# A hybrid decoder layer with product-key experts: sixteen more rows of the last dense tile take their down products from gathered expert rows, and the dense down products become 336 columns wide

## The chip, the cores and the metric

The kernel runs on one core of one Trainium2 chip. The metric is the device time of one execution in microseconds (us); the time before is 1582.34 us, the median of three runs (1581.97 to 1584.03). Everything is float32; a dense product is built from three TensorE products of the operands' high and low halves (high by high, high by low, low by high).

## The reference

The layer mixes 512 tokens of width 1024 through a gated convolution and an HGRN2 recurrence, attends to 256 memory tokens, and ends with the PEER channel mixer, which is where the change lies:

```python
q = (tokens @ w_query).reshape(Ntok, 8, 2, 128)
s = einsum('nhpd,hpkd->nhpk', q, sub_keys)          # 2 x 128 sub-keys per head
s_top, i_top = top_k(s, 16)
cand = s_top[:, :, 0, :, None] + s_top[:, :, 1, None, :]
best, pos = top_k(cand, 16)                          # 16 of 16384 experts per head
gate = softmax(best)
u = take(expert_down, idx);  a = gelu(einsum('nd,nhkd->nhk', x, u))
v = take(expert_up, idx);    out = einsum('nhk,nhkd->nd', gate * a, v)
```

So every token has 8 x 16 = 128 chosen experts; each costs one dot product with a row of `peer_down` (1024 numbers) and adds one weighted row of `peer_up`.

## The kernel before

The 512 tokens are four tiles of 128. The kernel splits them by method.

**Dense tokens.** For three tiles, less the last 32 rows of the third ("edge" rows), it computes all 16384 experts densely. `DN = 384` are the tokens of the three tiles, `DE = DN - EDGE = 352` those treated densely. The *down stage* runs over 128 blocks of 128 experts: `first_product(i)` calls `columns`, which does 8 x 3 = 24 matmuls with 352 moving columns into a PSUM bank; ScalarE applies GELU. 104 blocks of results are spilled to DRAM (`hid_dram`, ScalarE's DMA queue), 24 are kept. The *up stage* (`second_product`) again runs over 128 blocks, 24 matmuls of 352 columns each; its operand is the hidden value times a gate that is zero unless the token chose that expert.

**Gates.** The dense gate matrix is built by TensorE from one-hot matrices that VectorE makes. That is the *gate stage*: `STEPS = DE // TB = 44` steps of eight tokens. In step n VectorE makes the one-hots (`hots(n)`: two comparisons, one product), TensorE runs a down block and 24 small bf16 matmuls (`gate_step(n)`), ScalarE copies two banks of gates out. Before it run `AHEAD` down blocks, while VectorE still chooses experts; after it come the remaining down blocks, here called the *tail*.

**Gathered tokens.** For the fourth tile and the 32 edge rows, the expert rows are gathered. One gathered "row" is an indirect DMA by GpSimd (`down_row(k)`), which brings one expert row for each of 128 partitions (512 KB), and one VectorE instruction (`dots`, L1250 before) that multiplies it with the token in PSUM and sums. The fourth tile needs 128 such rows; the 32 edge tokens spread over four groups of 32 partitions, so 32 more: `ROWS = 160`. `row_stream` sets the order: 32 rows of the tile, the 32 of the edge, 96 of the tile. Whenever the kind changes, VectorE rewrites the token operand in PSUM (L1246, L1249). From the gate stage on four buffers hold the rows: row k is issued once the dot of row k-4 is done.

**What sets the order.** All is written out by hand. Per down block p: SyncE loads the weights (five buffers); ScalarE writes the high half (`high(p)`, L603) once block p-3 is done, since there are three buffers; GpSimd subtracts to get the low half (`low(p)`, L470); TensorE's block p waits for it. GpSimd has only one instruction stream, so gathers and low halves alternate in an order given by tables: `DOTS_STEP` says how many rows follow each low half in the gate stage (ten steps with two, then the pattern 1, 2, 2), `DOTS_END` how many follow each in the tail. VectorE's dots in the gate stage follow the same table. Edge data move between partitions by small DMAs on ScalarE's queue: tokens (`edge_h`), expert numbers (`edge_idx`, L889), gates (`edge_gate`, L918). At step `SPLIT_AT` VectorE splits the third tile's gates into three bf16 pieces (`gate_pieces`, L1374 to L1377).

## Time and profile before

| | us |
|---|---|
| median of three runs | 1582.34 |
| profiled execution, own time | 1584.32 |
| its span | 1582.4 |
| TensorE busy | 1565.8 (99% of the span) |
| VectorE busy | 1164.6 (74%) |
| GpSimd busy | 963.6 (61%) |
| ScalarE busy | 663.3 (42%) |

The down stage begins at 512.8 us into the span, its gate stage runs from 719.0 to 949.9, the tail to about 1073, the up stage to the end. TensorE is PE, VectorE DVE, ScalarE ACT, GpSimd POOL, SyncE SP. A matmul's listed duration overlaps that of the next, so the pace of TensorE is read from the distance of two starts, not from durations. A row of the timeline gives start, duration, engine, line, operation, output<-input, count, and in brackets how long the engine had been idle and what released it.

### The profile page before, as it was taken

How to read it: one execution, taken by the hardware profiler on the slowest of the kernel's cores; microseconds unless marked ns; L12 is line 12 of the kernel's file. 1: busy time of each engine (PE TensorE's matmuls, PEld its weight loads, DVE VectorE, ACT ScalarE, POOL GpSimd, SP SyncE). 2: the span in 40 equal slices, each digit the busy share in tenths (PEclk: the TensorE clock that was granted, in tenths of full speed). 3: DMA queues.
4: the chain of work that ended last, by engine and by line, in shares of the span. 5: the costliest groups of instructions: out<-in, count | busy, mean ns of one | idle time of the engine just before them, and what ended most of it. 6: DMA issues, size and time to landing. Idle time of an engine off the chain costs nothing.

```text
span 1582.4 us, 26079 instructions
## 1 busy us (share of the span) xinstructions
PE 1565.8 (99%) x9937; PEld 1483.6 (94%) x9937; DVE 1164.6 (74%) x2263; ACT 663.3 (42%) x994; POOL 963.6 (61%) x555
## 2 busy tenths in 40 slices
PE   8999999999999999999999999999999999999997
PEld 6888888888989999999999999999999999999997
DVE  5155351251579999999999883338999999998995
ACT  5352452552434444444444544334334333333433
POOL 4463326523235899887778778876757665564741
PEclk9999999999999999999999999999999999999999
DMA  5232252313424999989999999879999999999981
GB/s 196 88 103 67 73 158 95 115 54 118 149 84 130 302 347 349 330 285 313 379 399 397 396 410 393 309 248 365 411 410 406 399 406 409 395 404 393 400 354 54
DMA packets 129697, 438.91 MB, mean 277 GB/s; under 512 B 13888, under 2 KB 28224, under 8 KB 121280
## 3 DMA queue, kind: packets, MB, share of 16 engines
q1 hardware_dynamic: 60592, 227.43, 39.6%
q0 software_dynamic: 46080, 167.79, 27.8%
q10 hardware_dynamic: 22928, 42.41, 7.0%
q8 instruction: 59, 0.97, 0.2%
q14 instruction: 38, 0.31, 0.1%
HBM read 395.21 MB, written 41.81 MB: 276 GB/s over the span
## 4 chain that ended last, share of the span: by engine, by line
PE 50%; DVE 4%; DMA 3%; issue 1%; POOL 1%; ACT 0%; ACTq 0%; POOLq 0%
PE psum L1589 16%; PE psum L1590 16%; PE psum L1591 16%; DMA arena<-down_rows,kept 3%; PE psum L1905 2%; DVE arena L1415 1%; DVE arena L1250 1%; POOL w_low L470 1%; POOL arena L502 0%; DVE arena L1410 0%; DVE arena L1411 0%; DVE arena L1323 0%; DVE kept L1375 0%; DVE arena L1383 0%; PE psum L1941 0%
## 5 line engine op out<-in xcount | busy, mean ns | idle before, releaser
L470 POOL TENSOR_TENSOR w_low<-kept,w_high 128x1024 fp32r<-128x1024 f32 x205 | 500.7, 2445 | 316.8 <-ACT w_high L603 306.1
L1589 PE MATMUL psum<-hT_high,w_high 128*128 128x352 f32 (+2 forms) x1392 | 477.6, 343 | 1.7 <-POOL w_low L470 1.7
L1591 PE MATMUL psum<-hT_high,w_low 128*128 128x352 f32 (+2 forms) x1392 | 470.6, 338 | 0.0
L1590 PE MATMUL psum<-hT_low,w_high 128*128 128x352 f32 (+2 forms) x1392 | 470.6, 338 | 0.0
L1590 PE MATMUL psum<-wgt_low,up_high 128*128 128x352 f32 x1016 | 330.0, 325 | 0.0
L1589 PE MATMUL psum<-wgt_high,up_high 128*128 128x352 f32 x1016 | 328.7, 324 | 0.0
L1591 PE MATMUL psum<-wgt_high,up_low 128*128 128x352 f32 x1016 | 327.5, 322 | 0.0
L603 ACT ACTIVATE w_high<-kept 128x1024 fp32r<-128x1024 f32 x211 | 222.6, 1056 | 129.6 <-PE psum L1591 91.2
L1589 PEld LDWEIGHTS psum<-hT_high,w_high 128*128 128x128 f32 x1392 | 262.1, 188 | 14.5 <-issue 2.9
L1590 PEld LDWEIGHTS psum<-hT_low,w_high 128*128 128x128 f32 x1392 | 262.3, 188 | 11.8 <-issue 0.5
L1591 PEld LDWEIGHTS psum<-hT_high,w_low 128*128 128x128 f32 x1392 | 262.0, 188 | 12.0
L1250 DVE CUSTOM_DVE_ANT_0 arena<-arena,psum 128x1024 f32<-128x1024 f32 x160 | 192.3, 1215 | 78.1 <-DMA arena<-down_rows,kept 77.5
L607 ACT ACTIVATE up_high<-arena 128x1024 fp32r<-128x1024 f32 x128 | 135.6, 1059 | 269.2 <-PE psum L1591 214.8
L550 POOL DMA_INDIRECT kept<-up_in,kept x100 | 175.7, 1757 | 103.3 <-DVE kept L1459 76.0
L502 POOL DMA_INDIRECT arena<-down_rows,kept x160 | 153.2, 958 | 68.9 <-DVE kept L1250 45.8
L1591 PEld LDWEIGHTS psum<-wgt_high,up_low 128*128 128x128 f32 x1016 | 193.0, 190 | 0.0
L1590 PEld LDWEIGHTS psum<-wgt_low,up_high 128*128 128x128 f32 x1016 | 191.1, 188 | 0.0
L1589 PEld LDWEIGHTS psum<-wgt_high,up_high 128*128 128x128 f32 x1016 | 190.5, 188 | 0.0
L1445 DVE TENSOR_TENSOR up_low<-arena,up_high 128x1024 fp32r<-128x1024 f32 x128 | 156.4, 1222 | 20.0 <-ACT up_high L607 19.8
L550 POOL DMA_INDIRECT arena<-up_in,kept x60 | 112.4, 1873 | 66.6 <-DVE kept L1459 48.3
L1459 DVE SCALAR_TENSOR_TENSOR kept<-kept 128x1024 f32<-128x1024 f32 x80 | 102.4, 1280 | 2.0
L1415 DVE TENSOR_TENSOR arena<-arena,psum 128x3072 bf16<-128x3072 bf16 x44 | 76.9, 1748 | 0.0
(285 smaller groups left out, 1957.3 us busy)
## 6 DMA issues: line engine op xcount, KB each, us to landing
kept<-down_in SPq DMA_DIRECT2D x128, 512.0 KB, 6.4
arena<-up_pairs SPq DMA_DIRECT2D x64, 1024.0 KB, 9.2
kept<-front_w SPq DMA_DIRECT2D x92, 512.0 KB, 3.5
gate_dram<-arena ACTq DMA_DIRECT2D x40, 512.0 KB, 11.0
arena<-hid_dram SPq DMA_DIRECT2D x52, 352.0 KB, 12.7
arena<-gate_dram SPq DMA_DIRECT2D x8, 1280.0 KB, 14.0
kept<-gate_dram SPq DMA_DIRECT2D x8, 1280.0 KB, 14.2
hid_dram<-arena ACTq DMA_DIRECT2D x52, 176.0 KB, 6.6
```

Of the source, the lines that this page charges most:

```text
L470: nc.gpsimd.tensor_tensor(lower, ring[:, p % RING, :], high.bitcast(F32), ALU.subtract).then_inc(low_ready, 1)
L502: nc.gpsimd.indirect_dma_start(ring[slot], None, down_rows, bass.IndirectOffsetOnAxis((edge_idx if edge else idx3)[:, j:j + 1].bitcast(U32 ...
L550: nc.gpsimd.indirect_dma_start(rows_c[k % RING_C], None, up_rows, bass.IndirectOffsetOnAxis(numbers.bitcast(U32), 0))\
L603: nc.scalar.activation(w_half(p)[0], ring[:, p % RING, :], ACT.Copy).then_inc(high_ready, 1)
L607: nc.scalar.activation(up_hi[:, s % 4, :], uraw[:, up_slot(s), :], ACT.Copy).then_inc(up_high, 1)
L1250: nc.vector.tensor_tensor_reduce(ring[slot], ring[slot], h_row, 1.0, 0.0, ALU.mult, ALU.add, (edge_dot if edge else dot3)[:, j:j + 1]).the ...
L1415: nc.vector.tensor_tensor(hot_g[:, s], hot_i.rearrange("p (n q) i r -> p n q i r", q=1).to_broadcast(each), pieces[:, m:m + PAIRS].rearran ...
L1445: nc.vector.tensor_tensor(up_lo[:, up_slot(s), :], uraw[:, up_slot(s), :], up_hi[:, s % 4, :].bitcast(F32), ALU.subtract).then_inc(up_low, 1)
L1459: ins = nc.vector.scalar_tensor_tensor(x[:, ST, :], row, w3[:, n:n + 1], x[:, ST, :], ALU.mult, ALU.add)
L1589: nc.tensor.matmul(out, lhs[0], rhs[0], start=first, stop=False)
L1590: nc.tensor.matmul(out, lhs[0], rhs[1], start=False, stop=False)
L1591: return nc.tensor.matmul(out, lhs[1], rhs[0], start=False, stop=last)
```

## The change

`SEMI = 16` rows ahead of the 32 edge rows of the third tile leave the dense down products, which become `DS = DE - SEMI = 336` columns wide. The dense up products stay at 352. The 16 tokens are spread over eight groups of 16 partitions, so their 128 experts are 16 more gathered rows: `ROWS` goes from 160 to 176. They stand behind the edge rows in the stream. Their tokens, numbers and results travel by 24 more small DMAs on ScalarE's queue (8 for `semi_idx` with four blocks, 8 for `edge_h`, 8 for `semi_gel` with gate steps 17 to 20). Their GELU values are multiplied into the gates before these are split into pieces (now at step 23), so the dense gate matrix holds gate times GELU for them; in the up stage ScalarE copies these 16 columns per block (`weights_tail`) in place of VectorE's product. ScalarE's loop of the up stage is written out. The tables of times are shifted: `AHEAD` from 52 to 54.

```diff
-EXP_AT = (15, 30, 45)
-PICKED_AT = 19
-TURN_AT = (PICKED_AT + 4, 36, 52)
+EXP_AT = (16, 31, 47)
+PICKED_AT = 20
+TURN_AT = (PICKED_AT + 4, 38, 54)
...
+SEMI = 16
+DS = DE - SEMI
...
+SEMI_SLOTS = SLOTS // SEMI_PARTS
+ROWS = SLOTS + EDGE_SLOTS + SEMI_SLOTS
...
-GEL_AT, SPLIT_AT, LAST_TURN = 12, 20, 28
+GEL_AT, SEMI_AT, SPLIT_AT, LAST_TURN = 12, 17, 23, 30
...
-DOTS_END = (1,) * 22 + (2,) * 5
+DOTS_END = (2,) * 20 + (1,) * 8
...
+            def weights_tail(i):
+                block = (i + SPILL) % NK
+                nc.scalar.activation(wraw[:, i % 4:i % 4 + 1, DS:DE], near[:, block:block + 1, NEAR - SEMI:NEAR], ACT.Copy)\
+                    .then_inc(tail_copied, 1)
...
             def weight_high(i, s):
+                act.wait_ge(tail_copied, i + 1)
...
             for n in range(DT):
-                early_tiles((4 + PARTS, TURN_AT[0], TURN_AT[1])[n], EXP_AT[n])
+                if n == 1:
+                    act.wait_ge(edge_moved, 2 * 16 * PARTS)
+                    for q in range(SEMI_PARTS):
+                        if q % 2 == 0:
+                            early_at(TURN_AT[0] + q // 2)
+                        act.dma_start(semi_idx[q * SEMI:(q + 1) * SEMI, :],
+                                      idx_last[SEMI0:E0, q * SEMI_SLOTS:(q + 1) * SEMI_SLOTS]).then_inc(semi_moved, 16)
+                if n == 2:
+                    act.wait_ge(dot_done, FIRST_EDGE + 1)
+                    act.wait_ge(semi_moved, 16 * SEMI_PARTS)
+                    for q in range(SEMI_PARTS):
+                        early_at(TURN_AT[1] + q)
+                        act.dma_start(edge_h[q * SEMI:(q + 1) * SEMI], hn[SEMI0:E0, DT - 1, :].rearrange("p (k n) -> p k n", k=KC))\
+                            .then_inc(semi_moved, 16)
...
+                if n == SEMI_AT:
+                    act.wait_ge(dot_done, SEMI_DONE)
+                    act.wait_ge(semi_moved, 2 * 16 * SEMI_PARTS)
+                    step(nc.scalar.activation(semi_dot, semi_dot, ACT.Gelu))
+                if SEMI_AT <= n < SEMI_AT + SEMI_PARTS // 2:
+                    for q in (2 * (n - SEMI_AT), 2 * (n - SEMI_AT) + 1):
+                        act.dma_start(semi_gel[SEMI0:E0, q * SEMI_SLOTS:(q + 1) * SEMI_SLOTS],
+                                      semi_dot[q * SEMI:(q + 1) * SEMI, :]).then_inc(semi_moved, 16)
...
                     elif k == EDGE_DONE:
                         dve.wait_ge(dot_done, k)
+                        dve.wait_ge(semi_moved, 2 * 16 * SEMI_PARTS)
+                        step.put(nc.vector.memset(semi_gel, 1.0))
+                        step(nc.vector.tensor_tensor(h_chunks, edge_h, ffn_row.rearrange("p (k n) -> p k n", k=KC), ALU.mult))
+                    elif k == SEMI_DONE:
+                        dve.wait_ge(dot_done, k)
                         step(nc.vector.tensor_copy(h_chunks, own_h))
...
+                    dve.wait_ge(semi_moved, 3 * 16 * SEMI_PARTS)
+                    step.put(nc.vector.tensor_tensor(split_last[:, 2, :], split_last[:, 2, :], semi_gel, ALU.mult))
...
-                columns(i + FRONT, hT_half, DE, 4 + i % 2)
+                columns(i + FRONT, hT_half, DS, 4 + i % 2)
```

GpSimd near the end of the down stage, before: `w_low` is the low half of a down block's weights, `down_rows` a gathered row; one row follows each low half until the last three, which have two.

```order
253 L502 DMA arena<-down_rows,kept 128x1024 [waits dot_done]
254 L470 TENSOR_TENSOR w_low<-kept,w_high 128x1024 [waits high_ready]
255 L502 DMA arena<-down_rows,kept 128x1024 [waits dot_done] x2
256 L470 TENSOR_TENSOR w_low<-kept,w_high 128x1024 [waits high_ready]
259 L502 DMA arena<-down_rows,kept 128x1024 [waits dot_done] x2
260 L470 TENSOR_TENSOR w_low<-kept,w_high 128x1024 [waits high_ready] x7
```

The same place now, where the last of the low halves with two rows behind it stands; nineteen such pairs stand before it in the tail, and four with one row behind it.

```order
249 L476 TENSOR_TENSOR w_low<-kept,w_high 128x1024 [waits high_ready]
250 L510 DMA arena<-down_rows,kept 128x1024 [waits dot_done] x2
251 L476 TENSOR_TENSOR w_low<-kept,w_high 128x1024 [waits high_ready]
252 L510 DMA arena<-down_rows,kept 128x1024 [waits dot_done]
258 L510 DMA arena<-down_rows,kept 128x1024 [waits dot_done]
259 L476 TENSOR_TENSOR w_low<-kept,w_high 128x1024 [waits high_ready] x6
```

So in the tail twenty low halves have two gathers behind them where there were three. ScalarE behind the last copy of edge numbers (block 22 before, 23 now); `kept<-kept 32x32` is that copy, before:

```order
344 L855 DMA hid_dram<-kept 128x352 [waits gelu_out]
345 L889 DMA kept<-kept 32x32
346 L603 ACTIVATE w_high<-kept 128x1024 [waits block_used,weight_slot2]
347 L853 ACTIVATE kept<-psum 128x352 [waits hid_stored3,block_used]
348 L855 DMA hid_dram<-kept 128x352 [waits gelu_out]
```

and now:

```order
347 L869 DMA hid_dram<-kept 128x336 [waits gelu_out]
348 L917 DMA kept<-kept 32x32
349 L611 ACTIVATE w_high<-kept 128x1024 [waits block_used,weight_slot3,edge_moved]
350 L867 ACTIVATE arena<-psum 128x336 [waits hid_stored0,block_used]
351 L869 DMA hid_dram<-arena 128x336 [waits gelu_out]
352 L899 DMA kept<-kept 16x16 x2
```

The next high half of weights now also waits for `edge_moved`, that is for the landing of the copy issued just before it.

## Rows read from the trace of the kernel before

**Rows 1.** PE's waits over the whole span, the longest in the down stage.
```profile
PE psum L1589 <- POOL w_low L470: 1.9, 4, 1.1
```
**Rows 2.** Timeline, PE: moving widths 256 and 352.
```profile
224.90 0.28 PE L1591 MATMUL psum<-memT_high,w_low 128*128 128x256 f32 x1
...
225.62 0.28 PE L1591 MATMUL psum<-memT_high,w_low 128*128 128x256 f32 x1
...
999.94 0.32 PE L1589 MATMUL psum<-hT_high,w_high 128*128 128x352 f32 x1
...
1003.78 0.32 PE L1589 MATMUL psum<-hT_high,w_high 128*128 128x352 f32 x1
```
**Rows 3.** Timeline: ACT and POOL in one block of the tail.
```profile
1000.14 0.46 ACT L952 ACTIVATE arena<-psum 128x352 f32<-128x352 f32 x1 [2.43 <-PE psum L1591]
...
1001.62 2.41 POOL L470 TENSOR_TENSOR w_low<-kept,w_high 128x1024 fp32r<-128x1024 f32 x1 [0.34 <-ACT w_high L603]
```
**Rows 4.** Timeline: POOL in the tail, a block with two rows.
```profile
1028.51 2.40 POOL L470 TENSOR_TENSOR w_low<-kept,w_high 128x1024 fp32r<-128x1024 f32 x1 [0.33 <-ACT w_high L603]
...
1032.31 0.94 POOL L502 DMA_INDIRECT arena<-down_rows,kept  x1 [0.30 <-issue]
1033.27 2.41 POOL L470 TENSOR_TENSOR w_low<-kept,w_high 128x1024 fp32r<-128x1024 f32 x1
```
**Rows 5.** DMA issues, gathered rows, 950 to 975 and 1030 to 1045: count, median landing.
```profile
arena<-down_rows,kept POOLq DMA_INDIRECT x7, 8.0
...
arena<-down_rows,kept POOLq DMA_INDIRECT x6, 6.6
```
**Rows 6.** Timeline: ACT at the last copy of edge numbers; line L889's landings.
```profile
602.06 0.47 ACT L853 ACTIVATE kept<-psum 128x352 f32<-128x352 f32 x1 [1.27 <-PE psum L1591]
...
602.93 0.53 ACTq L889 DMA_DIRECT2D kept<-kept  x1
...
DMA to landing us min/median/max: 4.5/5.7/6.8
```
**Rows 7.** Timeline: DVE's first operation of the gate stage.
```profile
712.65 0.36 DVE L1406 COPY psum<-arena 128x192 f32<-128x192 f32 x1 [3.40 <-ACT arena L876]
```
**Rows 8.** Timeline: how a late row reaches PE in the gate stage.
```profile
774.81 1.22 DVE L1250 CUSTOM_DVE_ANT_0 arena<-arena,psum 128x1024 f32<-128x1024 f32 x1 [1.81 <-DMA arena<-down_rows,kept]
...
777.27 2.39 POOL L470 TENSOR_TENSOR w_low<-kept,w_high 128x1024 fp32r<-128x1024 f32 x1
...
779.81 0.40 PE L1589 MATMUL psum<-hT_high,w_high 128*128 128x352 f32 x1 [1.09 <-POOL w_low L470]
```
**Rows 9.** The chain that ended last: PE's small matmuls of two gate steps.
```profile
880.01 1.39 PE psum L1905 x24
885.29 1.39 PE psum L1905 x24
```
**Rows 10.** DVE by line, 719 to 950: count, busy us, mean ns; then L1246 alone.
```profile
L1250 DVE CUSTOM_DVE_ANT_0 arena<-arena,psum 128x1024 f32<-128x1024 f32 x76 | 91.1, 1218 | 11.2 <-DMA arena<-down_rows,kept 10.8
L1415 DVE TENSOR_TENSOR arena<-arena,psum 128x3072 bf16<-128x3072 bf16 x42 | 73.4, 1748 | 0.0
...
L1249 DVE COPY psum<-arena 128x1024 f32<-128x1024 f32 x1 | 1.2, 1220 | 0.0
...
L1246 DVE TENSOR_TENSOR psum<-arena x1: 2097/2097/2097, 637.4 to 637.4; 128x1024 f32<-128x1024 f32 x1
```
**Rows 11.** Timeline: DVE at the splitting of the gates.
```profile
815.05 3.20 DVE L1375 TENSOR_TENSOR kept<-kept 128x128 f32<-128x128 f32 x1
...
818.55 0.29 DVE L1377 TENSOR_TENSOR kept<-kept 128x128 f32<-128x128 f32 x1
```
**Rows 12.** Line L918, the four copies of edge gates in the gate stage.
```profile
DMA to landing us min/median/max: 7.5/9.0/11.9
```
**Rows 13.** Windows: us; PE, PEld, DVE, ACT, POOL busy; PE clock, DMA share, GB/s.
```profile
826.00:950.00 124.00, 123.73 (x1136) 120.66 (x1134) 111.67 (x150) 60.20 (x96) 98.00 (x66) 1.00 1.02 402
...
1576.00:1577.00 1.00, 0.00 (x0) 0.00 (x0) 1.00 (x3) 0.61 (x1) 0.00 (x0) 0.50 0.00 0
```

More of the change, by code:

```diff
@@ L85 @@
 SPILL = NK - KEEP
+OWN, AT_EDGE, IN_SEMI = range(3)
 def row_stream():
-    stream, own, edge = [], 0, 0
-    for k in range(ROWS):
-        if edge < EDGE_SLOTS and k >= FIRST_EDGE:
-            stream.append((True, edge))
-            edge += 1
-        else:
-            stream.append((False, own))
-            own += 1
-    return stream
+    middle = [(AT_EDGE, j) for j in range(EDGE_SLOTS)] + [(IN_SEMI, j) for j in range(SEMI_SLOTS)]
+    own = [(OWN, j) for j in range(SLOTS)]
+    return own[:FIRST_EDGE] + middle + own[FIRST_EDGE:]
 STREAM = row_stream()
 EDGE_DONE = FIRST_EDGE + EDGE_SLOTS
+SEMI_DONE = EDGE_DONE + SEMI_SLOTS
 V_MIX, V_CONV, V_HGRN, V_LB0, V_LB1, V_ATT, V_MEM, V_FFN, V_CW = 0, 8, 12, 16, 20, 24, 32, 40, 48
@@ L498, in down_row @@
                     pool.wait_ge(dot_done, k - ahead + 1)
-                edge, j = STREAM[k]
-                if edge and j == 0:
+                group, j = STREAM[k]
+                if group == AT_EDGE and j == 0:
                     pool.wait_ge(edge_moved, 2 * 16 * PARTS)
+                if group == IN_SEMI and j == 0:
+                    pool.wait_ge(semi_moved, 16 * SEMI_PARTS)
                 nc.gpsimd.indirect_dma_start(ring[slot], None, down_rows, bass.IndirectOffsetOnAxis(
-                    (edge_idx if edge else idx3)[:, j:j + 1].bitcast(U32), 0))\
+                    (idx3, edge_idx, semi_idx)[group][:, j:j + 1].bitcast(U32), 0))\
                     .then_inc(landed[slot], 16)
@@ L1241, in dots @@
                     dve.wait_ge(landed[slot], 16 * (n + 1))
-                    edge, j = STREAM[k]
+                    group, j = STREAM[k]
                     if k == FIRST_EDGE:
```

48 lines of the change are left out of this document (25 added, 23 removed).

## The prediction, on record before the changed kernel ran

> **What bounds the kernel now.** I read the page's table first: TensorE is busy 99% of the span. In the view of waits the longest entry that concerns the down stage is 1.9 us behind GpSimd's low halves, four times [rows 1]. So the time is TensorE's work, and a column less is worth its price as long as nobody else becomes late. Next that price: six matmuls of width 256 start 0.72 us apart (120.0 ns each), 24 of width 352 start 3.84 us apart (160.0 ns) [rows 2]. That is (160.0 - 120.0) / 96 = 0.417 ns a column; at 336 columns it gives 153.3 ns a matmul and 24 x 153.3 = 3.68 us a block. Then I asked, stage by stage, who would be late behind a faster TensorE. In a tail block TensorE begins a block at 999.94, ScalarE's GELU of the last one follows 0.20 later, then the high half, and the low half runs 1001.62 to 1004.03 [rows 2, 3]. The block that needs it starts two blocks after 999.94, at 1007.62: GpSimd leads by 3.6 us and can lead by no more, since the high half waits for a finished block. In the gate stage the chain is longer: a dot that waited 1.81 us for its row ends at 776.0, GpSimd's next low half starts at 777.27, TensorE's block at 779.81 after 1.09 us idle [rows 8]. VectorE and DMA are near their limits there: even in the calmer second half of the stage VectorE is busy 111.67 of 124 us and the DMA share is 1.02 at 402 GB/s [rows 13].
>
> **The change, part by part.** The sum is made against the profiled execution, 1584.3 us (span 1582.4 and 1.9 around it), which is 2.0 above the median of the runs.
>
> *Width.* 128 blocks x 24 = 3072 matmuls lose 16 x 0.417 = 6.67 ns each: -20.5 us. Both widths of the slope bracket nothing near 336 but the line; I give this term no range.
>
> *The tail.* `DOTS_END` puts two gathers behind twenty low halves. Such a block takes GpSimd 1033.27 - 1028.51 = 4.76 us [rows 4], and the two behind it in the trace the same within 0.05; it waits for no other engine in it. TensorE will want a block each 3.68 us. Before, 22 tail blocks had one gather (2.41 for the low half and some 1.1 for the gather, hidden in 3.84), three had two, and the lead swallowed those 3 x 0.92. Now GpSimd loses 4.77 - 3.68 = 1.09 us on each of twenty, 21.8 us, of which the lead, 7.36 - 4.09 = 3.3 us at the new pace, swallows its part once: TensorE waits 18.5 us. Nothing repays it. That is the lower end. The upper end comes from the four row buffers: row k needs the dot of row k-4, so a pair of rows needs half of landing L plus dot and gaps, about (L + 1.6) / 2. With the 6.6 us at the tail's end this is 4.1, hidden; with the median of 8.0 at its start, where the spill and the last gate stores still run, it is 4.8, and 5.5 for a row that takes 9.4 [rows 5]. If all twenty blocks went at 5.5 it would be 33 us. The first six have that load; I add 2 us for them and take 20.5 (18.5 to 33).
>
> *A new wait on ScalarE, once.* After the fourth copy of edge numbers ScalarE waits until it has landed; behind that wait stand the high half of block 26, hence GpSimd's low half and TensorE's block. The copy is issued 0.87 us after the GELU starts, and such copies land after 4.5 to 6.8 us, 5.7 in the middle [rows 6]. From the start of block 24: 0.20 + 0.87 + 5.6, then high half and gap 1.12 (in rows 3 the 1.48 from GELU to low half, less 0.36 of GELU), low half 2.41: 10.2 us, where TensorE wants it at 2 x 3.68 = 7.36. Stall 2.8 us (1.7 to 4.1). Could the start of the gate stage swallow it? There VectorE waits 3.40 us for the turned indices [rows 7], so it isn't the late one, and the stall stays.
>
> *Gate steps 2 to 11.* The bubble of rows 8 falls in step 11: up to there VectorE, its rows and GpSimd set the pace, and TensorE's lead is used up. What TensorE saves by then is lost again: 12 x 0.16 = 1.9 us. VectorE also gets a product of tokens and norm gains (2.10 us for L1246) in place of the copy (1.22), and a small memset [rows 10]: +1.0. Together 2.9 us (1.9 to 4; the copy itself comes back at step 16, when VectorE gains: steps with one dot).
> By the Trainium skill ("SBUF — State Buffer", Who interferes with whom), a VectorE operation with both inputs in SBUF and a GpSimd operation that reads SBUF exclude each other. The trace fits: the subtraction L1375 took 3.20 us, its twin L1377 0.29 [rows 11]; by the rule that product would cost the 1.2 us of the copy where GpSimd is idle, and the term would be 1.9.
>
> *The split at step 23.* VectorE must now have all of `semi_gel`, whose last two copies are issued with step 20, behind its block. Let T be the start of step 20's small matmuls. ScalarE's GELU is at T + 0.2, the second copy's issue at about T + 1.65, its landing, by the nearest copies in this stage, 9.0 us later (7.5 to 11.9) [rows 12]: T + 10.7. VectorE would be there some 5 us earlier, since its one-hots of step 22 can start once step 19's matmuls are done. It then splits in about 1.5 us, for GpSimd, held by missing dots, is idle (before, L1375 alone took 3.20 [rows 11]), makes the one-hots of step 23 (the longest 1.75, together some 2.9) and two dots of 1.15 [rows 10]: T + 17.4. From a dot's end to TensorE's block it is 3.8 us [rows 8]: T + 21.2. A step takes 5.28 now [rows 9], 5.12 after, so the unstalled block would come at T + 3 x 5.12 + 1.36 = 16.7. Stall 4.5 us, less some 0.5 that the splitting cost TensorE before (its 1.9 us of waits less the bubbles at step 11): 4.0. From below, if the copies land at once and the split waits for a low half again, 1; from above, late landings and a late ScalarE, 8.
>
> *Rest.* The up stage keeps its width. ScalarE gets one copy of 16 columns a block; it is busy 42% and mostly waits for TensorE there, so nothing (0 to 1). Spill and its reload shrink by 8 KB a block: nothing. Gaps may lower the clock: the granted clock is 1.00 through the gate stage and 0.50 (1.2 GHz) at 1576, when TensorE has stopped [rows 13]. At half clock a block costs 3.7 us more. For the two gaps of 3 to 4 us I take 0.5 (0 to 4).
>
> Sum: -20.5 + 20.5 + 2.8 + 2.9 + 4.0 + 0.5 = +10.2 us. Against 1584.3 that is 1594.5, against the median 1592.5. All lower ends give +2.6, all upper ones some +34.
>
> **The rivals.**
> *Faster: TensorE's width decides and the gathers stay hidden.* For it: TensorE waits for nobody now, and GpSimd is idle 39% of the span. It would need GpSimd's two-gather block under 3.68 + 3.3 / 20 = 3.85 us; rows 4 say 4.76. Price: -20.5 and some 2 us of gate-stage stalls, 1564. Chance 0.06.
> *No change: the tail eats the gain and the rest is absorbed.* The copies of edge numbers land early, the gate stage recovers in its steps with one dot, and little but the 18.5 is paid: -20.5 + 18.5 + about 2, so 1580 to 1585. Against it: a stall of TensorE is never repaid, and the steps up to 11 have no slack. Chance 0.15.
> *Slower still: the four row buffers pace the tail.* If rows land after 9 us all through, a block takes 5.3 to 5.5 us, the tail term is 29 to 33 and the time 1601 to 1605. It decides from a landing of about 8 us on. Against it: with 1.5 MB in 4.77 us the tail moves some 330 GB/s once the spill ends, below the 402 of the gate stage [rows 13]. Chance 0.15.
> *The clock falls in the gaps.* In the tail TensorE would idle 1.1 of each 4.8 us, and twice for 3 to 4. If a long gap led to 1.2 GHz, one or two blocks after each would take 7.4 in place of 3.68: +4 to +11 us, 1596 to 1603. The trace has a gap of 1.09 [rows 8] in a stage whose clock stays 1.00. Chance 0.07. The Trainium skill ("TensorE: Matmul & The Clock Gate", HAM oscillation) has such gaps cost a kernel its warm clock; by it the ScalarE wait and the split threaten, not the tail. No run here shows it yet.
>
> **How the numbers follow.** The forecast has 0.57, the rivals 0.06, 0.15, 0.15 and 0.07. About 0.2% (3.2 us) is what a measurement tells from no change, so 1579.1 to 1585.5 is "same". Faster gets the first rival and a fifth of the second, 0.09; same gets the rest of the second and a little of the forecast's low end, 0.13; slower 0.78. The range leaves out the first rival and the far end of the third: 1582 to 1605.
>
> **What would show it.** In the profile after: matmuls of the down stage 153.3 ns apart where they run unhindered; in the tail TensorE's blocks 4.8 us apart for about twenty blocks, each wait released by GpSimd's low half, TensorE busy about 77% there; one gap of about 3 us near 610 us behind ScalarE's wait for `edge_moved`; VectorE idle for some 5 us ahead of the split and a gap of TensorE behind it; an up stage of the same length. It would be wrong in the main if the tail ran at 3.7 us a block, that is if GpSimd's block with two gathers took clearly less than 4.7 us; and wrong in size if the row buffers or the clock took part.

## The result, and the profile after

| | before | after |
|---|---|---|
| median, us (4 runs each) | 1582.3 | 1605.55 |
| all runs | 1582.0 to 1584.0 | 1605.1, 1605.3, 1605.8, 1611.8 |
| profiled execution (span) | 1584.3 (1582.4) | 1605.1 (1603.4) |
| ratio, 95% interval | | 1.0154 (1.0128 to 1.018) |

The kernel is slower, as forecast, but by 23 us and not by 10: half a microsecond outside the range. The whole difference lies in the down stage (560.1 us before, 581.3 after); the up stage took 509.5 and 509.3.

Where is it? The trace has all 3072 matmuls of the down products, so the start of each of the 128 blocks can be read off, and a stage's length less its matmuls at full pace is what TensorE lost there. A block's work is 3.84 us before and 3.68 after, a gate step's small matmuls 1.36. Some 3.7 us of the gate column are the restart behind each of these (0.09 each) and about 0.6 is one turning of indices, both in every kernel. In the last row the 0.5 us that the prediction set aside for the clock is halved between the first two columns.

| lost, us | ahead of the gates | gate stage | tail | sum |
|---|---|---|---|---|
| before | 2.7 | 6.0 | 0.1 | 8.8 |
| after | 11.7 | 9.0 | 29.7 | 50.5 |
| difference | 9.0 | 3.0 | 29.6 | 41.7 |
| forecast | 3.0 | 7.2 | 20.5 | 30.7 |

41.7 less 20.5 for the width is the 21.2 us of the stage. Against the forecast the tail is 9.1 over, the part ahead of the gates 6.0 over, and the gate stage 4.2 under. So the width did what it should: nine matmuls in 1.38 us, 153.3 ns each (timeline of PE after; start and duration first):

```profile
833.82 0.32 PE L1629 MATMUL psum<-hT_high,w_high 128*128 128x336 f32 x1
...
835.20 0.32 PE L1629 MATMUL psum<-hT_high,w_high 128*128 128x336 f32 x1
```

PE's waits after, for the line of [rows 1] (us in total, times, longest):

```profile
PE psum L1629 <- POOL w_low L476: 32.2, 26, 4.8
```

The tail, for [rows 4]: POOL's two gathers and low half repeat every 4.76 us without a wait for anyone, and PE waits 0.84 us in each.

```profile
991.43 0.39 PE L1629 MATMUL psum<-hT_high,w_high 128*128 128x336 f32 x1 [0.84 <-POOL w_low L476]
991.45 0.95 POOL L510 DMA_INDIRECT arena<-down_rows,kept  x1 [0.16 <-issue]
992.70 0.94 POOL L510 DMA_INDIRECT arena<-down_rows,kept  x1 [0.30 <-issue]
993.66 2.39 POOL L476 TENSOR_TENSOR w_low<-kept,w_high 128x1024 fp32r<-128x1024 f32 x1
996.21 0.95 POOL L510 DMA_INDIRECT arena<-down_rows,kept  x1 [0.16 <-issue]
```

That law (4.77 us a block, 1.09 lost) holds for twelve of the blocks 98 to 117. But blocks 99 to 103 took 5.5 to 5.7 us, and blocks 113 to 115 took 6.99, 5.30 and 5.85. And the lead of 3.3 us that I took off was not there: already at the tail's second block PE waited, because GpSimd had itself waited for a dot product just before.

```profile
955.32 0.94 POOL L510 DMA_INDIRECT arena<-down_rows,kept  x1 [2.16 <-DVE kept L1288]
956.28 2.39 POOL L476 TENSOR_TENSOR w_low<-kept,w_high 128x1024 fp32r<-128x1024 f32 x1
958.81 0.39 PE L1629 MATMUL psum<-hT_high,w_high 128*128 128x336 f32 x1 [0.86 <-POOL w_low L476]
```

Landings of the gathers, for [rows 5], from the DMA issues of 954 to 976 and of 1019 to 1022 (count, KB, median us to landing):

```profile
arena<-down_rows,kept POOLq DMA_INDIRECT x8, 8.8
...
arena<-up_pairs SPq DMA_DIRECT2D x1, 1024.0 KB, 8.9
...
arena<-down_rows,kept POOLq DMA_INDIRECT x2, 10.0
```

The new wait on ScalarE, for [rows 6]. The copy landed after some 7.6 us, not 5.6, and TensorE stood 4.85 us:

```profile
603.50 0.52 ACTq L917 DMA_DIRECT2D kept<-kept  x1
611.18 1.06 ACT L611 ACTIVATE w_high<-kept 128x1024 fp32r<-128x1024 f32 x1 [8.09 <-DMA kept<-kept]
612.32 2.35 POOL L476 TENSOR_TENSOR w_low<-kept,w_high 128x1024 fp32r<-128x1024 f32 x1 [5.71 <-ACT w_high L611]
614.82 0.62 PE L1629 MATMUL psum<-hT_high,w_high 128*128 128x336 f32 x1 [4.85 <-POOL w_low L476]
```

Windows, for [rows 13] (same columns): the gap did not end the loss. Behind it TensorE ran at 0.52, that is nearly all at 1.2 GHz, some 22 matmuls 0.28 us apart; in 40 us of the tail, with a gap of 0.84 us in each block, it stayed at 1.00.

```profile
614.80:621.00 6.20, 6.18 (x23) 6.20 (x24) 5.95 (x31) 1.89 (x3) 5.70 (x5) 0.52 0.61 198
...
975.60:979.00 3.40, 3.38 (x13) 3.40 (x14) 2.19 (x3) 0.24 (x1) 2.35 (x3) 0.53 1.03 420
990.00:1030.00 40.00, 32.43 (x199) 30.19 (x199) 18.20 (x31) 12.41 (x18) 35.54 (x25) 1.00 0.93 337
```

The split of step 23, for [rows 11]: VectorE waited for the small copies, GpSimd for its dot product, PE for the low half.

```profile
840.53 0.29 DVE L1469 TENSOR_TENSOR kept<-kept 128x128 f32<-128x128 f32 x1 [3.68 <-DMA kept<-kept]
...
846.27 0.95 POOL L510 DMA_INDIRECT arena<-down_rows,kept  x1 [6.06 <-DVE kept L1288]
...
851.00 0.39 PE L1629 MATMUL psum<-hT_high,w_high 128*128 128x336 f32 x1 [2.62 <-POOL w_low L476]
```

### The profile page after: what moved, and what is told of

It reads as the page before. It is cut to its first block, busy times and chain, and to the rows that moved or that the text cites. A ratio compares the mean times of both kernels' runs of the same rounds, so it can differ in the third digit from the quotient of the medians.

```text
span 1603.4 us, 26095 instructions
## 1 busy us (share of the span) xinstructions
PE 1555.7 (97%) x9937; PEld 1469.1 (92%) x9937; DVE 1181.2 (74%) x2298; ACT 674.4 (42%) x1123; POOL 941.0 (59%) x571
## 4 chain that ended last, share of the span: by engine, by line
PE 42%; DVE 6%; DMA 6%; POOL 4%; issue 2%; ACT 0%; ACTq 0%
PE psum L1629 14%; PE psum L1630 13%; PE psum L1631 13%; DMA arena<-down_rows,kept 5%; POOL w_low L476 2%; DVE arena L1453 2%; DVE arena L1288 2%; POOL arena L510 2%; PE psum L1945 1%; DVE arena L1448 1%; DVE arena L1449 1%; DMA kept<-kept 0%; DVE psum L1279 0%; DVE arena L1361 0%; PE psum L1981 0%
## 5 line engine op out<-in xcount | busy, mean ns | idle before, releaser
L1629 PE MATMUL psum<-hT_high,w_high 128*128 128x336 f32 (+2 forms) x1392 | 473.8, 340 | 32.0 <-POOL w_low L476 32.0
L1631 PE MATMUL psum<-hT_high,w_low 128*128 128x336 f32 (+2 forms) x1392 | 465.2, 334 | 0.0
L1630 PE MATMUL psum<-hT_low,w_high 128*128 128x336 f32 (+2 forms) x1392 | 465.0, 334 | 0.0
L1630 PEld LDWEIGHTS psum<-hT_low,w_high 128*128 128x128 f32 x1392 | 263.9, 190 | 11.9 <-issue 0.5
L1288 DVE CUSTOM_DVE_ANT_0 arena<-arena,psum 128x1024 f32<-128x1024 f32 x176 | 211.2, 1215 | 76.6 <-DMA arena<-down_rows,kept 76.3
L558 POOL DMA_INDIRECT kept<-up_in,kept x100 | 155.0, 1550 | 125.7 <-DVE kept L1499 98.0
L510 POOL DMA_INDIRECT arena<-down_rows,kept x176 | 167.9, 954 | 79.6 <-DVE kept L1288 52.5
L558 POOL DMA_INDIRECT arena<-up_in,kept x60 | 95.7, 1595 | 80.9 <-DVE kept L1499 61.6
L619 ACT ACTIVATE arena<-arena 128x16 f32<-128x16 f32 x128 | 27.5, 215 | 246.7 <-PE psum L1631 246.5
```

The lines of the kernel that those rows point to most:

```text
L510: nc.gpsimd.indirect_dma_start(ring[slot], None, down_rows, bass.IndirectOffsetOnAxis((idx3, edge_idx, semi_idx)[group][:, j:j + 1].bitcas ...
L558: nc.gpsimd.indirect_dma_start(rows_c[k % RING_C], None, up_rows, bass.IndirectOffsetOnAxis(numbers.bitcast(U32), 0))\
L1288: nc.vector.tensor_tensor_reduce(ring[slot], ring[slot], h_row, 1.0, 0.0, ALU.mult, ALU.add, (dot3, edge_dot, semi_dot)[group][:, j:j + 1] ...
L1629: nc.tensor.matmul(out, lhs[0], rhs[0], start=first, stop=False)
L1630: nc.tensor.matmul(out, lhs[0], rhs[1], start=False, stop=False)
L1631: return nc.tensor.matmul(out, lhs[1], rhs[0], start=False, stop=last)
```

## The experiments

Medians; the kernel before, run beside them each time, lay at 1583.1 to 1584.0, against 1582.3 beside the changed kernel, so ratios compare better than medians. The changed kernel has 1.0154 (1.0128 to 1.018). The intervals of w1, s1, w2, w3, t1, t3, u1 and t4 overlap with it: by time alone none of these is told from the changed kernel, and what is said of them rests on the traces. "Lost" is from the one profiled run of each, as in the table above. p1 leaves out the down products of 16 tokens, r1 sixteen gathered rows and their dot products.

| kernel | us | ratio to before, 95% | lost: ahead, gates, tail |
|---|---|---|---|
| p1: before, width alone | 1576.6 | 0.9951 (0.9935 to 0.9968) | 8.7, 8.6, 3.7 |
| p2: changed, wide again | 1617.1 | 1.0211 (1.0194 to 1.0228) | 4.5, 11.9, 25.5 |
| r1: changed, 16 gathers fewer | 1580.4 | 0.9973 (0.9961 to 0.9986) | 11.3, 14.4, 4.6 |
| w1: wait later | 1611.3 | 1.0164 (1.0138 to 1.0189) | 7.9, 17.7, 30.5 |
| s1: split at step 26 | 1607.4 | 1.0151 (1.0131 to 1.017) | 11.5, 11.0, 31.0 |
| w2: both | 1603.8 | 1.0125 (1.0107 to 1.0143) | 8.4, 11.8, 30.3 |
| w3: w2, slower rate ahead | 1602.8 | 1.0119 (1.0102 to 1.0136) | 9.1, 9.0, 30.6 |
| t1: mixed order in the tail | 1604.4 | 1.0136 (1.0119 to 1.0153) | 10.0, 11.6, 26.9 |
| t3: seven row buffers | 1602.2 | 1.0111 (1.0086 to 1.0135) | 10.8, 15.9, 24.0 |
| u1: up loads later | 1604.1 | 1.0141 (1.0126 to 1.0156) | 11.9, 9.9, 27.6 |
| t4: t1, low halves on VectorE | 1600.3 | 1.0108 (1.0077 to 1.0139) | 11.7, 15.1, 21.0 |
| v2: t4 and w2 | 1598.2 | 1.0087 (1.0067 to 1.0106) | 7.9, 10.4, 23.3 |
| v3: v2, seven buffers, rate | 1587.5 | 1.0026 (1.0013 to 1.0038) | 9.0, 8.5, 14.7 |
| v4 | 1580.4 | 0.9981 (0.9972 to 0.999) | 3.2, 9.1, 11.4 |
| v5 | 1584.6 | 1.0005 (0.9991 to 1.0019) | 2.5, 11.8, 7.1 |
| v6 | 1582.8 | 0.9996 (0.9983 to 1.0009) | 2.7, 9.5, 13.1 |
| v7 | 1583.9 | 0.9997 (0.9987 to 1.0007) | 2.3, 8.8, 18.4 |
| v8 | 1578.4 | 0.9964 (0.995 to 0.9977) | 3.2, 11.1, 7.9 |

**The width alone, the width undone, the rows undone.**

```diff
-                columns(i + FRONT, hT_half, DE, 4 + i % 2)        # p1, in before
+                columns(i + FRONT, hT_half, DE - 16, 4 + i % 2)
-                columns(i + FRONT, hT_half, DS, 4 + i % 2)        # p2, in changed
+                columns(i + FRONT, hT_half, DE, 4 + i % 2)
-ROWS = SLOTS + EDGE_SLOTS + SEMI_SLOTS                            # r1, in changed
+ROWS = SLOTS + EDGE_SLOTS
-DOTS_END = (2,) * 20 + (1,) * 8
+DOTS_END = (1,) * 24 + (2,) * 2
```

> The kernel before, with the down products 336 columns wide and nothing else changed (16 tokens' down products are left out). Theory: 128 blocks x 0.16 us = 20.5 us less work of TensorE, of which GpSimd (one gather per block, 3.5 us, in most of the tail) gives back 2 to 4 us before the gate stage and in the last blocks with two gathers: 1563 to 1566 us. Rival: GpSimd at 1.2 gathers per block and at one per block with a 3.68-us block is already the bound, and half of the width's gain is lost: 1570 to 1574.

> The changed kernel with its down products 352 columns wide again (the 16 more columns are computed and thrown away); all gathers, waits and orders as changed. Theory: GpSimd's work and the landings bound blocks 7 to 118, TensorE only the other 17 and part of the gate stage; the 0.16 us per block mostly fill time that TensorE waited: 1607 to 1613 us. Rival (my prediction's way of adding): the width is worth its 128 x 0.16 us wherever the rows stand, less only the 20 blocks with two gathers: 1605.5 + 17 = 1622.5, range 1620 to 1625.

> The changed kernel without the last 16 gathered rows of the fourth tile and their dot products (left out of the result), so 28 gathers are left for the tail, one per block for 24 blocks and two for 2. Theory: a block with one gather takes GpSimd 3.54 us and hides behind TensorE's 3.68, a second one costs 1.09 us; 18 fewer such blocks give 19.6 us back, the late row 3.8 and the late start 2 to 4: 1578 to 1581 us. Near the kernel with the narrow width alone (1576.6), so the wait and the splitting are worth little. Rival: the change's other parts (wait, splitting, copies) hold a good half of the loss, and this is 1588 to 1592.

p1 was the surprise: 20.5 us less work of TensorE, only 7.4 us less time, less even than the rival said. Without a single row more, the loss grew by 6.0, 2.6 and 3.6 us in the three stages. Its timeline of POOL shows the first of these:

```profile
604.02 2.41 POOL L470 TENSOR_TENSOR w_low<-kept,w_high 128x1024 fp32r<-128x1024 f32 x1
606.59 0.96 POOL L502 DMA_INDIRECT arena<-down_rows,kept  x1 [0.16 <-issue]
607.57 2.41 POOL L470 TENSOR_TENSOR w_low<-kept,w_high 128x1024 fp32r<-128x1024 f32 x1
610.14 1.10 POOL L502 DMA_INDIRECT arena<-down_rows,kept  x1 [0.16 <-issue]
611.54 0.94 POOL L502 DMA_INDIRECT arena<-down_rows,kept  x1 [0.30 <-issue]
612.50 2.41 POOL L470 TENSOR_TENSOR w_low<-kept,w_high 128x1024 fp32r<-128x1024 f32 x1
615.06 0.39 PE L1589 MATMUL psum<-hT_high,w_high 128*128 128x336 f32 x1 [0.49 <-POOL w_low L470]
```

A block with one gather takes GpSimd 3.55 us, one with two 4.8 to 4.9. Ahead of the gates every fifth block has two: 4 x 3.55 + 4.76 = 18.96 us (19.13 with the 4.93 of this row), hidden behind five blocks of 3.84 (19.2), not behind five of 3.68 (18.4). So PE waited 0.4 to 0.7 us in blocks 16, 21, 26, 31 and 41, which with the restart behind each is 3.8 of the 8.7 us lost ahead of the gates. Of the 3.7 us lost in the tail 2.2 are at blocks 119 to 121, behind the three low halves with two gathers. At 352 columns GpSimd was just fast enough, and my reading of it as idle 39% of the span hid that. p2 says the same from the other side: 16 columns more cost 11.5 us where the rows stand (1617.1 against 1605.55; some 9 by the ratios), which lies between the two theories (2 to 8, and 15 to 20) and bears out neither. r1 came at the forecast number. In its tail the blocks with one gather ran at 3.68 us, its loss fell from 29.7 to 4.6; but its profiled run (1585.2) had the long case of the split (below) and a new gap of 2.7 us at block 126, so the other parts of the change are not nothing. Between r1 and the changed kernel lie 25.2 us for 16 gathers: this is the run that shows the gathers to be the main cause.

**The wait, the split, the rate.** w1 puts two more blocks ahead of ScalarE's wait; s1 sets `SPLIT_AT` to 26; w2 has both; w3 adds the rate.

```diff
-                    act.wait_ge(edge_moved, 2 * 16 * PARTS)       # w1
                     for q in range(SEMI_PARTS):
+                        if q == 0:
+                            early_tiles(TURN_AT[0], TURN_AT[0] + LATER)
+                            act.wait_ge(edge_moved, 2 * 16 * PARTS)
...
-                while k < DOTS_A and k - RING_A < (i - FIRST_DOT) * 6 // 5:     # w3
+                while k < DOTS_A and k - RING_A < (i - FIRST_DOT) * 21 // 20:
```

> The changed kernel, with ScalarE's wait for the landing of the edge numbers two blocks later (two more high halves and GELUs ahead of it). Theory: the wait alone made both TensorE's gap behind block 24 (5.0 us) and the 22 matmuls at 1.2 GHz after it (2.7 us), so both go: 1605.5 - 7.7 = 1597.8 us, and no matmul of the down stage before the gates is at half clock. Rival 1: the low clock has another cause and stays, at this or another place: 1600.5. Rival 2: the copies of the numbers, now two blocks later, or GpSimd, whose lead was restored by the stall, make a new stall: above 1602.

> The changed kernel, with the splitting of the gates at step 26 in place of 23, and so 15 us more for the eight small copies of GELU values. Theory: VectorE's wait for their landing (3.68 us in the profiled run of the changed kernel, 7.07 us in that of the kernel with seven row buffers) goes; with it goes 2.8 us at block 78 in the short case, and 9.4 us less 1 in the long one, which made some runs 6 us longer: 1602 to 1603.5 us, and the runs lie within 3 us of each other. Rival: GpSimd is behind anyway, and the bubble only moves to another block: 1604.5 to 1606, the spread of the runs as before (1605.1 to 1611.8).

> The last kernel, with ScalarE's wait for the edge numbers two blocks later too. The later wait alone gave 1611.3 us, with the long case of the split in its profile. Theory: GpSimd's work is what bounds blocks 7 to 118, and TensorE's stall of 7.7 us had only given GpSimd time that it needs later; without the stall 4 us came back ahead of the gate stage and 2 at step 11: so 1600 to 1602 us, 1 to 2 under the kernel with the split alone. Rival: the later wait was masked by the long case only, and is worth its 7.7 us: 1594 to 1596.

> The kernel with the later wait and the later split (1603.8 us), with GpSimd's gathers ahead of the gate stage spread as 21 in 20 blocks in place of 6 in 5. Theory: the bubbles of 0.45 to 0.5 us in every fifth block (16, 21, 26, ... 52) and 2 us at block 37 are the second gather, which makes GpSimd's five blocks 18.9 us long against TensorE's 18.4; they go, and the gate stage begins 3 to 4 us earlier: 1600 to 1601.5 us. Rival: VectorE now waits for rows that come later, its choosing ends later, and the gate stage begins no earlier: 1603 to 1607.

The gap and the slow matmuls at block 26 were gone in w1, as the theory said, and the time did not fall. Half came back before the gates (the loss ahead fell by 3.8, not 7.7): GpSimd, no longer given 5 us, was late at blocks 33, 36 and 37. More came back in the gate stage, and there I found what scatters these kernels. In w1 and in t3 the copies landed later still (VectorE waited 8.35 and 7.07 us). The chain from the landing over the dot product and the low half to TensorE made block 77 11.8 us long, where it took 7.9 in the changed kernel, and block 78, partly at half clock, took 1.4 (t3) or 2.7 us (w1) more than its due. Below I call this the long case of the split. t3's rows, against the 3.68, 6.06 and 2.62 above:

```profile
845.21 0.29 DVE L1481 TENSOR_TENSOR kept<-kept 128x128 f32<-128x128 f32 x1 [7.07 <-DMA kept<-kept]
850.95 0.95 POOL L518 DMA_INDIRECT arena<-down_rows,kept  x1 [9.44 <-DVE kept L1300]
855.67 0.62 PE L1641 MATMUL psum<-hT_high,w_high 128*128 128x336 f32 x1 [4.53 <-POOL w_low L481]
```

t3's four runs were 1598.8, 1599.1, 1605.4 (the profiled one) and 1606.4: that the two low ones are the short case is likely from the 6 us, but they have no trace. s1 took the landing away and was no faster. Its VectorE waited for nobody at the split, and then this:

```profile
853.68 0.94 POOL L510 DMA_INDIRECT arena<-down_rows,kept  x1 [1.50 <-DVE kept L1288]
854.04 3.11 DVE L1412 TENSOR_SCALAR kept<-kept 128x128 uint32<-128x128 uint32 x1
...
854.64 2.41 POOL L476 TENSOR_TENSOR w_low<-kept,w_high 128x1024 fp32r<-128x1024 f32 x1
...
862.33 0.95 POOL L510 DMA_INDIRECT arena<-down_rows,kept  x1 [5.28 <-DVE kept L1288]
```

An operation that took 0.23 us in the changed kernel took 3.11 here and ended 0.1 us behind GpSimd's low half. In the changed kernel it had run while GpSimd stood idle for lack of dot products: the wait for the landing had spared it this one. The Trainium skill ("SBUF — State Buffer", Who interferes with whom) gives the shared pair of ports, which an operation like this one can take, to whichever of the two engines issues first and blocks the other for the whole instruction. The trace agrees that VectorE was blocked. It agrees less plainly on the order: VectorE's operation is listed 0.60 us ahead of the low half, though behind the start of GpSimd's gather issue. w3's bubbles of every fifth block went (52 blocks in 193.7 us against w2's 199.2), and TensorE met VectorE, which chooses experts up to there:

```profile
713.93 0.29 DVE L1418 TENSOR_TENSOR arena<-psum,arena 128x128 f32<-128x128 f32 x1
714.27 1.33 PE L1994 MATMUL psum<-kept,arena 128*128 128x128 f32 x5 [3.53 <-DVE arena L1418]
```

So the first gate step began 0.6 us later in w3 than in w2 in their profiled runs. w2, with both, was 3.6 us under s1 by the medians, more than the 1 to 2 expected and half of the 7.7 of the rival; the two intervals overlap. In these runs each wait taken away was followed by another close behind it.

**The tail: order, buffers, loads.** t1 has `DOTS_END = (2, 2, 2, 1) * 5 + (2,) * 6 + (1,)`; t3 three more row buffers from the seventh gather on; u1 the up loads 8 blocks later.

```diff
+        rows_d = rows_b + [at(188 + 4 * j, D) for j in range(RING_D - RING_B)]     # t3; 7 - 4
...
-                if g < 2:                                               # u1
-                    load_ups(pair_of(2 * g), 2 * g)
+                if g >= 2:
+                    load_ups(pair_of(2 * g - 4), 2 * g - 4)
```

> The changed kernel, with the same 48 gathers in the tail in another order: five times (2, 2, 2, 1), six times 2, once 1 in place of twenty times 2, eight times 1. Theory: the tail is bound by GpSimd's own work, the sum of low halves and issues, which is the same, so the loss stays: 1603 to 1607 us, with 21 blocks 4.77 us apart. Rival: a good part of the loss (8 of 29.7 us) comes from gathers in an unbroken row of twos, four buffers and landings of 8 to 10 us; blocks with one gather between them give the buffers time: 1596 to 1600 us.

> The changed kernel, with seven row buffers in place of four from the seventh gather of the tail on (the three more stand where the first ring had them; the first gates of the up stage are loaded once the last dot is done). Theory: twenty blocks with two gathers keep GpSimd's 4.77 us each; what came on top, 3.8 us at the late row (block 114 to 116) and about 2 us behind the first blocks, goes: 1599 to 1601 us. Rival 1: the four buffers paced the whole tail: the blocks come nearer than 4.77 us and the time falls below 1592. Rival 2: they paced nothing, the late row is the transfer itself: 1604 to 1607.

> The changed kernel, with SyncE's first two loads of up weights (1 MB each) issued 8 blocks later, at block 120 and 124 in place of 112 and 116. Theory: the late row of blocks 113 to 116 (landings of 9.1 and 10.1 us, gaps of 3.1 and 2.0 us, 12 matmuls at 1.2 GHz) is these loads in front of the gathers on the DMA queues; it goes, and the kernel is 3.8 to 5 us faster, 1600.5 to 1602 us, as it was with seven buffers. Rival: the landing times vary by themselves (the same place was late in six kernels, but with the same loads), and the gap moves: 1604.5 to 1606.

t1 stayed, as GpSimd's sum of work says. (The rows run out before the tables do: 44 gathers follow in the tail, not the 48 of the expectation, with two behind 20 low halves in the changed kernel and behind 19 here.) In t3's profiled run the blocks from 101 to 117 were all 4.77 us (4.76 to 4.78); its tail lost 24.0, 5.7 less, as expected. So the four buffers paced blocks 101 to 103 and the late row. Blocks 99 and 100, ahead of the new buffers, still took 5.5. u1 names the late row. With the 1-MB load of up weights out of the way the gathers issued from 1019 to 1023 landed in 5.6 us (median of two, as is the 10.0), and blocks 113 to 117 took 4.77 each:

```profile
arena<-down_rows,kept POOLq DMA_INDIRECT x2, 5.6
```

Only 2.1 us of it reached the tail's sum, since its first blocks lost more in this run and a gap of 1.3 us opened at block 126. The median fell by 1.5, too little to be told from noise.

**Relieving GpSimd.** VectorE makes eleven of the tail's low halves.

```diff
+BY_DVE = range(DURING + 1, DURING + 22, 2)
-                low(FRONT + i)
+                if i not in BY_DVE:
+                    low(FRONT + i)
...
+                if i in BY_DVE:                                         # VectorE's stream
+                    high, lower = w_half(position(FRONT + i))
+                    dve.wait_ge(high_ready, FRONT + i + 1)
+                    nc.vector.tensor_tensor(lower, ring[:, position(FRONT + i) % RING, :], high.bitcast(F32), ALU.subtract)\
+                        .then_inc(dve_low, 1)
...
```

> The changed kernel with the mixed order of the tail, and VectorE, idle for half of the tail, makes eleven of its low halves (every other block from 99 to 119; 1.22 us each there against GpSimd's 2.40). Theory: GpSimd's own work is the bound of the tail: it falls by 11 x 2.4 = 26 us, the tail comes down from 138.6 us (this order without it) to 113 to 120, and the time to 1580 to 1586. Rival 1: the DMA queues are the bound (they moved 412 GB/s at share 1.03; two gathers and a block of weights in 3.68 us are 427 GB/s): blocks with two gathers 4.2 us or more apart, 1592 or more. Rival 2: the two engines keep each other from the memory, as the 3.20-us subtraction of before shows, and half of the gain is lost: 1590 to 1594.

> The changed kernel with all of it: the later wait, the split at step 26, the mixed order of the tail and eleven low halves on VectorE. Theory: the sum of the parts, 1605.5 - 2.8 (split) - 1 to 2 (wait) - 20 to 24 (tail) = 1577 to 1582 us, a little under the kernel before (1584.0 in the last runs). Rival: without the stalls ahead GpSimd enters the tail later, and the tail gives 15 only: 1586 to 1588.

> The kernel with all (later wait and split, mixed order, eleven low halves on VectorE: 1598.2 us), with seven row buffers in the tail and 21 gathers in 20 blocks ahead of the gates. Theory: with GpSimd relieved the tail is held by four buffers times landings of about 8 us (it waits up to 2.3 us for a dot product, and this for a landing); three more buffers take the bubbles of 13 us down by two thirds, the rate gives 2 to 3: 1586 to 1590 us. Rival: the DMA queues themselves are full (share 0.97 to 0.99 in that stretch) and more buffers only make the landings longer: 1594 to 1597.

t4 and v2 missed by some 15 us. GpSimd's work was no longer the bound; it waited for a dot product, and that for a landing, since four buffers turn over no faster:

```profile
987.61 0.93 POOL L513 DMA_INDIRECT arena<-down_rows,kept  x1 [2.32 <-DVE kept L1292]
988.56 2.37 POOL L479 TENSOR_TENSOR w_low<-kept,w_high 128x1024 fp32r<-128x1024 f32 x1
989.32 1.22 DVE L1292 CUSTOM_DVE_ANT_0 arena<-arena,psum 128x1024 f32<-128x1024 f32 x1 [1.98 <-DMA arena<-down_rows,kept]
991.07 0.62 PE L1641 MATMUL psum<-hT_high,w_high 128*128 128x336 f32 x1 [3.55 <-POOL w_low L479]
```

The rival of my prediction, buffers that pace the tail, is borne out from here on: with seven of them (v3) the loss in the tail fell by 8.6 us more. v3 also has the slower rate, but that ends ahead of the gates.

**The last four moves.** v4 takes v3 with `AHEAD` 55, 9 gathers in 8 blocks ahead, u1's loads, `DOTS_END = (2, 2, 2, 2, 2, 1) * 4`, and the first weights of the up stage at block `NK - 3`. v5 lets VectorE's dots of the tail stand one block later behind its low halves. v6 and v7 are v5 and v4 with the up loads early again; v8 is v5 with the second up load behind the first gates.

> The kernel with all, seven buffers and the slower rate (1587.5 us), with four more moves: the gate stage one block later (55 down blocks ahead, since VectorE ended its choosing 4.0 us after TensorE wanted it) with 9 gathers in 8 blocks, the up loads of the first pairs later, the first weights of the up stage one block later (ScalarE waited there for VectorE, 3.5 us at block 127), and the tail's gathers as four times (2, 2, 2, 2, 2, 1). Theory: 4 to 5 us from the first, 3.5 from the third, 1 from the others: 1577 to 1580 us, faster than the kernel before (1583.9) by 0.3%. Rival: each gap closed opens the next one of GpSimd and the landings, as the wait and the split did: 1582 to 1586.

> The last kernel, with VectorE's low halves of the tail one block of dot products earlier from block 104 on (from there it makes a low half before it waits for the gathers that were issued two blocks before). Theory: the waits of TensorE for VectorE's low halves (2.7 us at block 105, 1.5 at 117, each with a dot product that waited for its landing right before it) go: 3 to 5 us under the last kernel, 1573 to 1576. Rival: GpSimd then waits longer for the dot products to free the buffers, and its own low halves come late instead: no change or slower, 1577 to 1582.

> The kernel v5 with the first loads of up weights back at blocks 112 and 116. In v5's profiled run TensorE stood 9.3 us ahead of the up stage: the first gates were loaded once the last dot product was done, behind a 1-MB load of up weights, and landed after 12 us; its tail up to there was 3 us shorter than v4's. Theory: with the up loads early again the gates land in 6 to 7 us as in the kernel with seven buffers, and nothing else moves, since seven buffers cover the late row: 1575 to 1578 us. Rival: the gates' landing varies by itself and the up loads don't matter: 1582 to 1586, with a spread of 10 us as in v5.

> The kernel v4 with the same step back. Theory: as for v6, and VectorE's low halves still wait for landings: 1578 to 1580.5 us, 2 to 3 over v6. Rival: v4 lost nothing to the up loads, and the late row of blocks 113 to 116 comes back: 1581 to 1584.

> The kernel v5 (up loads late) with the second of its two up loads behind the first gates instead of in front of them. Theory: in v5 the gates landed 12 us after their issue, behind 1 MB of up weights, and TensorE stood 9.3 us; alone on the queues they land in 6 to 7, and the stall falls to 3 or less, while the late row stays away: 1577 to 1580 us with a spread under 8 us. Rival: the gates' landing is not set by that load, and this is v5 again: 1582 to 1586.

v4 is faster than the kernel before (by 0.1 to 0.28%); which of its moves did it was not taken apart. v5's tail lost least, as expected, and its median was worse: TensorE stood at the start of the up stage, for gates that landed 12 us after their issue.

```profile
1059.76 0.65 SPq L397 DMA_DIRECT2D arena<-gate_dram  x1
...
1071.84 0.49 DVE L1542 TENSOR_TENSOR arena<-arena 128x320 f32<-128x320 f32 x1 [11.88 <-DMA arena<-gate_dram]
...
1074.62 0.66 PE L1997 MATMUL psum<-wgt_high,up_high 128*128 128x384 f32 x1 [9.32 <-DVE wgt_low L1553]
```

v6 and v7 failed their theory: with the up loads early the gates landed in 6.3 and 7.0 us, but the tail lost 6 and 7 us more than in v5 and v4 (v7's blocks 117 and 118 took 6.79 and 6.42), so u1's mechanism holds with seven buffers too. v8 has both, late up loads, and the gates ahead of the second of them:

```profile
1057.30 0.65 SPq L397 DMA_DIRECT2D arena<-gate_dram  x1
...
1064.48 0.49 DVE L1543 TENSOR_TENSOR arena<-arena 128x320 f32<-128x320 f32 x1 [6.96 <-DMA arena<-gate_dram]
...
1067.26 0.41 PE L1998 MATMUL psum<-wgt_high,up_high 128*128 128x384 f32 x1 [1.32 <-DVE wgt_low L1554]
```

That the load in front was what delayed v5's gates is not shown: v4 has the same loads in the same order, its load was issued 8.9 us ahead of the gates where v5's was some 12.4 ahead, and its gates landed in 6.3 us. v8's five runs lie within 3.7 us (v5's twelve within 12.8), and at 1578.4 us it beats both kernels: 0.36% (0.23 to 0.50) under the one before, 27 us under the changed one. No run gives the kernel before the same late loads, buffers and low halves on VectorE, so how much of the 0.36% is due to the narrower products stays open. Of the 7.9 us that v8 still loses in the tail 6.2 are in blocks 100 and 101: a gap of 3.5 us behind a low half that waited for a dot product and its landing, then half clock. From 968 to 1050 it lost little more, with most blocks 3.68 us apart beside two gathers each, at a DMA share of 1.03:

```profile
962.29 0.62 PE L1658 MATMUL psum<-hT_high,w_high 128*128 128x336 f32 x1 [3.51 <-POOL w_low L486]
...
962.30:968.00 5.70, 5.70 (x21) 5.70 (x22) 3.60 (x5) 0.00 (x0) 3.77 (x4) 0.53 1.03 417
968.00:1050.00 82.00, 80.97 (x527) 80.38 (x526) 54.68 (x82) 31.51 (x44) 70.33 (x51) 1.00 1.03 412
```

## Why the prediction was right or wrong

- *Width, -20.5:* right as work (153.3 ns a matmul). Wrong as a term that could be added without a range: alone it was worth 7.4 us (p1), because GpSimd's one or two gathers a block no longer hid behind it everywhere. In the changed kernel this shows less ahead of the gates: of the 9.0 us there 7.7 are ScalarE's wait, and the stall at block 26 gave GpSimd time back (in w1, without the stall, the waits at blocks 33, 36, 37 and 41 came or grew).
- *Tail, 20.5; measured 29.6.* This is the step that failed. Twenty blocks at 4.77 us, each lost to GpSimd's second gather: right. The deduction of 3.3 us "of which the lead swallows its part once" was wrong; I took the lead from the middle of a calm tail, while this tail begins behind a gate stage in which GpSimd had just waited 2.16 us for a dot. The 2 us for late landings were 4.0, in blocks 99 to 103; and 3.8 at blocks 113 to 115 weren't in the sum at all: SyncE's 1-MB up loads stand in the same queues (u1), and [rows 5] gave only a median for 1030 to 1045. 21.7 + 4.0 + 3.8 = 29.5. Two stretches at half clock lie inside these terms: that at block 114 made 1.5 of the 3.8; that at block 102 seems hidden, for the block took 5.46 like its neighbours.
- *ScalarE's wait, 2.8; measured 7.7.* The mechanism and place were right, the size not: the copy landed 2 us later than the middle of [rows 6], outside its 4.5 to 6.8; and 2.7 us came from matmuls at 1.2 GHz, which I had priced at 0.5 for the whole kernel. Yet taking the wait away gave nothing alone (w1), and by the medians 3.6 us beside the later split (s1 and w2).
- *Gate steps 2 to 11, 2.9, and the split, 4.0; measured together 3.0.* Over-sized in the profiled run: the steps up to 11 lost 0.7 more than before, not 2.9, and the split's bubble was 2.8, which is 2.3 more than before. In the profiled runs of t3 and w1 that bubble came to 8.1 and 9.4, at and over the upper bound of 8 that I gave.
- *Rivals.* The four buffers do not pace the changed kernel's tail (t3: 4.77 us a block with seven as well), although the time came within 0.6 us of where that rival put it, 1601 to 1605: right time, wrong reason. The clock rival had the right signs (three stretches at half clock, some 5.7 us together), at a chance of 0.07 for the whole of it.
- *The sum.* 30.7 us of losses forecast, 41.7 measured. The sign was forecast for the right main reason, GpSimd's second gather. Most of the misses came from prices of things taken one by one where they share GpSimd, VectorE and the DMA queues.

Left open: why VectorE waits 3.4 us and more longer for the eight small copies in some runs, and whether a split kept clear of both the landing and GpSimd's low half would pay.

## What to carry to other kernels

Before you credit a faster bottleneck with its full gain, compute the period of the next engine over its real pattern (here five blocks: 18.96 us against 19.2 and then 18.4), not its share of the span. A wait that appears beside a saturated helper may be free, because the helper uses it; test by removing it before you mend it. And look in the stage you change for every large transfer that shares its queues: moving one load behind the gates (v5 to v8) was worth 6.2 us by the medians, nearly the 7.4 that the 16 columns gave alone.

## What the runs showed of the hardware

- After a gap of 4.85 us TensorE's clock was 0.52 of full over the next 6.2 us (changed kernel). Three gaps of 1.6 to 1.8 us, 5.5 apart, were followed by 3 us at 0.53 (975.6), a single one of 2.6 us at 851.0 by none, and nine of 0.84, one in each block, by none: the granted clock from 990 to 1030 was 1.00. This is milder than the oscillation of which the Trainium skill warns ("TensorE: Matmul & The Clock Gate", HAM oscillation): no stretch at the low clock in the down stage of any kernel here lasted longer than some 22 matmuls.
- Not only VectorE is slowed when both work at once. While VectorE made a low half in t4 (1.22 us), GpSimd's issue of a gather took 1.76 us, where it takes 0.95 (and 0.94 to 0.96 beside VectorE's dot products alone):

```profile
999.27 1.22 DVE L1484 TENSOR_TENSOR w_low<-kept,w_high 128x1024 fp32r<-128x1024 f32 x1 [0.72 <-ACT w_high L615]
999.56 1.76 POOL L513 DMA_INDIRECT arena<-down_rows,kept  x1 [0.16 <-issue]
```

- VectorE makes the same low half in 1.22 us for which GpSimd takes 2.40, when it doesn't meet one of GpSimd's. Where it did, in v4, it took 3.03, and GpSimd's next gather issue took 1.76:

```profile
981.12 2.39 POOL L485 TENSOR_TENSOR w_low<-kept,w_high 128x1024 fp32r<-128x1024 f32 x1
981.58 3.03 DVE L1499 TENSOR_TENSOR w_low<-kept,w_high 128x1024 fp32r<-128x1024 f32 x1
983.67 1.76 POOL L522 DMA_INDIRECT arena<-down_rows,kept  x1 [0.16 <-issue]
```

- The landing of one and the same transfer can differ by a factor of two: a 512-KB gather 5.6 us without and 10.0 with the 1-MB load in front (u1 against the changed kernel), 1.25 MB of gates 6.3 (v4), 7.0 (v8) or 11.9 (v5).
